# Scores of the cross-attention's heads placed between its query projections

## The chip, the core and the metric

The kernel runs on one core of one Trainium2 chip. The metric is the device time of one execution in microseconds (us). The engines are TensorE (PE; PEld is its weight load, which overlaps), VectorE (DVE), ScalarE (ACT), GpSimd (POOL) and SyncE (SP), which only issues transfers here. Each engine runs its own queue of instructions in order and waits on semaphores that the others raise.

## The reference, cut to what matters

A decoder trunk of two layers over 256 tokens of width 1024. Each layer has a mixer of four head groups, a cross-attention into 256 memory tokens, and a grouped mixture of experts, each followed by a LayerNorm. The change is in the cross-attention:

```python
def memory_cross_attention(x, mem, wq, wk, wv, wo):
    q = (x @ wq).reshape(bsz, s_len, X_HEADS, X_HEAD_DIM)      # 4 heads of 256
    k = (mem @ wk).reshape(bsz, -1, X_HEADS, X_HEAD_DIM)
    v = (mem @ wv).reshape(bsz, -1, X_HEADS, X_HEAD_DIM)
    s = jnp.einsum('bqhd,bkhd->bhqk', q, k).astype(jnp.float32) * (X_HEAD_DIM ** -0.5)
    p = jax.nn.softmax(s, axis=-1).astype(v.dtype)
    o = jnp.einsum('bhqk,bkhd->bqhd', p, v).reshape(bsz, s_len, D_MODEL)
    return o @ wo
```

## The kernel before

**Units.** Every large weight matrix is cut into units of 1 MB. A unit is loaded by SP into one of six `raw` slots, split by ACT into a rounded high half (`hi`, L618: `w_hi`, two instructions) and by DVE into the remainder (`lo`, L903: `w_lo`, two instructions), and used by PE in three products for each pair of operands (L1490 to L1492, `three`). There are two split slots. `ahead(u)` on ACT and on DVE splits unit u+2 as soon as PE has used unit u. The cross-attention of a layer has four value units (`U_V`), four query units (`U_Q`, one for each head: `project("xq0")` to `project("xq3")`) and four output units (`U_O`). SP loads a unit when the unit before it in the same slot has been split; loads of the expert weights follow in the same queue.

**A head of the cross-attention.** `xq{h}`: the query unit, moved out of PSUM by ACT to `qT` (`move`, L641). `cs{h}`: its scores, on PE at L1739, each of four products run as two passes. `x_head_max(h)` on DVE (L1260) gives the row maxima and raises `xmax_ready`. The exponentials on ACT (L782) write `xprobs` and, by a read of the accumulator, the row sums. DVE takes the reciprocal (L1268), multiplies (L1271) and raises `xprobs_ready`. `cpt{h}`: PE transposes the probabilities (L1748, `x_probs_t`), ACT moves them to `xprobsT` (L641). `cpv{h}`: PE multiplies by the values (L1760), ACT moves the result (L641), and DVE splits it (`split_y`, L933 and L935) for the output units, which accumulate in `quad` (L1490 to L1492). In the trace `qT`, `xprobs`, `xprobsT` and the values all show as `arena`, and the keys as `mem_kT`.

**What sets the order.** The order on each engine is written out by hand. PSUM results other than the long accumulations go through four banks (`ring`): `ring_jobs()` lists the jobs of a layer in order with the engine that empties each, job i uses bank i mod 4, and `free` makes PE wait until job i-4 has been emptied. The waits count the jobs that an engine has emptied, so each engine must keep to the order of the list.

**Order before.** PE runs the four query units, then the scores of heads 0 to 3, then `cpt0`, and then for each head `cpt{h+1}` and `cpv{h}`, then the output units. ACT moves `xq0` to `xq3`, with a split (`hi`) after each, and then has the exponentials of heads 0 to 3, `cpt0`, `cpt1`, `cpv0` and so on. DVE splits three units (`lo` of the third and fourth query unit and of the first output unit), then works through maxima and multiplications, and then splits the second output unit.

Of the kernel before, what the change touches and what calls it, by code (L numbers as in the profile page):

```python
# [23 lines left out]
X_HEADS = 4  # L24
# [33 lines left out]
U_Q = U_V + 4  # L58
# [14 lines left out]
def ring_jobs():  # L73

    jobs = [(f"xa{i}", "dve") for i in range(4)]
    jobs += [("cq", "act"), ("ckv", "dve"), ("v", "act"), ("ssq", "dve"), ("ssk", "dve"), ("u", "act"),
             ("rb0", "dve"), ("b", "act")]
    jobs += [(f"q{i}", "act") for i in range(4)]
    jobs += [("kn0", "act"), ("kn1", "act"), ("vv0", "act"), ("vv1", "act"), ("d", "act")]
    jobs += [(f"qt{i}", "act") for i in range(4)]
    jobs += [("wst", "act"), ("c", "act"), ("s0", "act"), ("s1", "act"), ("s2", "act"), ("s3", "act"), ("h", "act")]
    jobs += [(f"mt{i}", "dve") for i in range(4)]
    jobs += [("pt0", "act"), ("pt1", "act"), ("s4", "act"), ("s5", "act"), ("xk0", "act"), ("pv0", "dve"), ("mix", "dve"), ("pt2", "act"), ("pt3", "act"), ("s6", "act"),
             ("s7", "act"), ("xk1", "act"), ("pv1", "dve"), ("pt4", "act"), ("pt5", "act"), ("xk2", "act"),  # L90
             ("yd", "dve"), ("pv2", "dve"), ("pt6", "act"), ("pt7", "act"), ("pv3", "dve"), ("xk3", "act")]
    jobs += [(f"xb{i}", "dve") for i in range(4)]
    jobs += [(f"xq{i}", "act") for i in range(4)]
    jobs += [(f"cs{i}", "act") for i in range(4)]
    jobs += [("cpt0", "act")]
    for i in range(4):
        jobs += ([(f"cpt{i + 1}", "act")] if i < 3 else []) + [(f"cpv{i}", "act")]
    jobs += [("xc0", "act"), ("xc1", "act"), ("rt0", "act"), ("xc2", "act"), ("xc3", "dve"), ("rt1", "act")]
    jobs += [(f"gb{i}", "act") for i in range(8)]
    return jobs  # L100


def hybrid_trunk_kernel(nc, x, mem, positions, w_in, gmlp_v_norm_g, gmlp_w_s, gmlp_b_s, mla_q_norm_g,
# [57 lines left out]
    with ExitStack() as ctx:  # L161
# [114 lines left out]
        xb_hi = rounded("xb_hi", 9216, DC, SEQ)  # L276
        xb_lo = rounded("xb_lo", 0, DC, SEQ)
# [66 lines left out]
        values_moved = sem("values_moved")  # L344
# [259 lines left out]
        def _(act):  # L604
# [85 lines left out]
            for l in range(DEPTH):  # L690
                def ahead(u):

                    hi(u + SPLIT_SLOTS, l, size.get(u + SPLIT_SLOTS, NORMAL))
# [20 lines left out]
                for i in range(4):  # L714
                    t, h = i // 2, 4 * (i % 2)
# [10 lines left out]
                for i in range(4):  # L726
                    t, h = i % 2, 4 * (i // 2)
# [45 lines left out]
                    for a in range(2):  # L773
                        last = nc.scalar.copy(xv[:, t, 512 * a:512 * a + 512], quad[:, 2 * t + a, :])
                last.then_inc(values_moved, 1)
                for i in range(4):
                    move(f"xq{i}", l, qT[:, 2 * i:2 * i + 2, :], bank2(f"xq{i}"), scale=256.0 ** -0.5, unit=U_Q + i)
                    ahead(U_Q + i)
                for h in range(X_HEADS):
                    act.wait_ge(xmax_ready, l * X_HEADS + (h + 1))  # L780
                    for t in range(T):
                        nc.scalar.activation(xprobs[:, h, 256 * t:256 * t + 256],  # L782
                                             bank(f"cs{h}")[:, 256 * t:256 * t + 256], ACT.Exp,
                                             bias=smax[:, h, t:t + 1], accum_out=ssum[:, h, t:t + 1])
                    act.drain().then_inc(act_emptied, 1)
                def x_probs_t(h):
                    if h >= 2:
                        act.wait_ge(misc_ready, misc_done(f"cpv{h - 2}", l))
                    move(f"cpt{h}", l, xprobsT[:, h % 2, :], bank(f"cpt{h}"))

                x_probs_t(0)
                for h in range(X_HEADS):
                    if h + 1 < X_HEADS:
                        x_probs_t(h + 1)

                    move(f"cpv{h}", l, qT[:, 2 * h:2 * h + 2, :], bank2(f"cpv{h}"))
# [101 lines left out]
        def _(dve):  # L898
# [130 lines left out]
            for l in range(DEPTH):  # L1029
# [10 lines left out]
                def ahead(u):  # L1040
                    lo(u + SPLIT_SLOTS, l, size.get(u + SPLIT_SLOTS, NORMAL))
# [211 lines left out]
                x_low("xb", l, 2, None, xb_hi, xb_lo)  # L1253
                for i in range(2, 4):
                    ahead(U_V + i)
                for i in range(3):
                    ahead(U_Q + i)
                def x_head_max(h):
                    dve.wait_ge(misc_ready, misc_done(f"cs{h}", l))
                    nc.vector.tensor_reduce(smax[:, h, :], bank2(f"cs{h}"), AX_X, ALU.max, negate=True)  # L1260
                    dve.drain().then_inc(xmax_ready, 1)

                x_head_max(0)
                for h in range(X_HEADS):
                    if h + 1 < X_HEADS:
                        x_head_max(h + 1)
                    dve.wait_ge(act_emptied, emptied(f"cs{h}", l))
                    nc.vector.reciprocal(srec[:, h, :], ssum[:, h, :])  # L1268
                    dve.drain()
                    for t in range(T):  # L1270
                        nc.vector.tensor_scalar(xprobs[:, h, 256 * t:256 * t + 256], xprobs[:, h, 256 * t:256 * t + 256],  # L1271
                                                srec[:, h, t:t + 1], None, ALU.mult)
                    dve.drain().then_inc(xprobs_ready, 1)
                ahead(U_Q + 3)
                for h in range(X_HEADS):
                    dve.wait_ge(act_emptied, emptied(f"cpv{h}", l))
# [197 lines left out]
        def _(pe):  # L1474
# [106 lines left out]
            for l in range(DEPTH):  # L1581
# [60 lines left out]
                for i in range(2):  # L1642
                    o = free(f"kn{i}", l)
                    for j in range(4):
                        h = 4 * i + j
# [82 lines left out]
                        transpose_x("xb", l, 1)  # L1728
                    into_quad(x_hi, x_lo, 2 * i, 2, U_V + i, l, i == 0, i == 3, values=True)
                pe.wait_ge(dve_emptied, emptied("xb3", l))  # L1730
                for i in range(4):
                    project(f"xq{i}", U_Q + i, l, xb_hi, xb_lo)
                pe.wait_ge(values_moved, l + 1)
                for h in range(X_HEADS):
                    o = free(f"cs{h}", l)
                    pe.wait_ge(act_emptied, emptied(f"xq{h}", l))
                    for t in range(T):
                        for c in range(2):
                            r = mm(o[:, t * 256:(t + 1) * 256], qT[:, 2 * h + c, t * P:(t + 1) * P], kT[:, 2 * h + c, :],  # L1739
                                   start=c == 0, stop=c == 1)  # L1740
                    r.then_inc(misc_ready, 1)
                def x_probs_t(h):
# [6 lines left out]
                                                    ident[:])  # L1749
                    r.then_inc(misc_ready, 1)  # L1750

                x_probs_t(0)
                for h in range(X_HEADS):
                    if h + 1 < X_HEADS:
                        x_probs_t(h + 1)
                    o = free(f"cpv{h}", l)
                    pe.wait_ge(act_emptied, emptied(f"cpt{h}", l))
                    for c in range(2):
                        for m in range(2):
                            r = mm(o[:, c * SEQ:(c + 1) * SEQ], xv[:, m, 256 * h + 128 * c:256 * h + 128 * c + P],  # L1760
                                   xprobsT[:, h % 2, 256 * m:256 * m + 256], start=m == 0, stop=m == 1)
                    r.then_inc(misc_ready, 1)
# [301 lines left out]
```

## Time and profile before

| | |
|---|---|
| median of 3 runs | 774.19 us (770.89 to 776.81) |
| the profiled execution, its own time | 775.23 us |
| span of its core, first to last instruction | 773.4 us |
| mean granted TensorE clock | 0.979 of full speed |
| PE busy | 727.7 us, 94% of the span |
| DVE busy | 400.7 us, 52% |
| ACT busy | 276.4 us, 36% |

The profiled execution takes 1.8 us more than its span; that is what lies before the first and behind the last instruction. Times in the rows are counted from the start of the span. The cross-attention's query units of layer 0 run from 171.7 us, those of layer 1 from 550.2 us.

### The profile page before, as it was taken

To read this page: it belongs to the slowest core of one execution; us is meant where nothing else is said; L and a number is where in the kernel's file an instruction comes from. 1 tells how busy PE (TensorE), PEld (TensorE's weight loads), DVE (VectorE), ACT (ScalarE), POOL (GpSimd) and SP (SyncE) were. 2 spreads that over 40 slices of the span, in tenths; PEclk is the share of its full clock that TensorE was granted. 3 is DMA by queue.
4 is the path that set the end of the run, shared out by engine and by line. 5 is a ranking of instruction groups with operands and counts; after the bars stand their busy time and mean duration, and the time that the engine had idled before them with its cause. 6 is when DMAs were issued, how large, how long until landed. Compare 5 with 4: busy or idle time off the path is not lost.

```text
span 773.4 us, 12363 instructions
## 1 busy us (share of the span) xinstructions
PE 727.7 (94%) x4972; PEld 591.5 (76%) x4972; DVE 400.7 (52%) x701; ACT 276.4 (36%) x473; POOL 46.4 (6%) x88
## 2 busy tenths in 40 slices
PE   3999999999999989999799989999999999899992
PEld 3989897889789965655499789888997898565651
DVE  4685886664537612111558587858444573111115
ACT  4355643444524122111334565335553231211121
POOL 3500000010004200000020000001000010000000
PEclk8999999999999999999999999999999999999996
DMA  8991334573329479999975322456631573899961
GB/s 274 345 316 57 120 124 164 175 244 127 108 91 364 150 278 389 417 415 416 347 262 165 111 96 84 149 184 220 196 109 56 217 328 114 325 412 418 418 271 57
DMA packets 62496, 176.11 MB, mean 228 GB/s; under 512 B 3824, under 2 KB 37024, under 8 KB 53216
## 3 DMA queue, kind: packets, MB, share of 16 engines
q1 hardware_dynamic: 57824, 162.80, 57.0%
q0 software_dynamic: 4032, 12.24, 4.9%
q8 instruction: 43, 0.70, 0.4%
q10 hardware_dynamic: 576, 0.20, 0.1%
q14 instruction: 21, 0.17, 0.1%
HBM read 174.18 MB, written 1.05 MB: 227 GB/s over the span
## 4 chain that ended last, share of the span: by engine, by line
PE 85%; DVE 7%; issue 2%; ACT 2%; DVEq 2%; DMA 1%; ACTq 0%; POOL 0%; POOLq 0%; SPq 0%
PE ring L1882 14%; PE ring L1490 7%; PE ring L1915 7%; PE ring L1491 7%; PE ring L1492 7%; PE quad L1490 6%; PE quad L1491 6%; PE quad L1492 6%; PE quad L1927 4%; PE ring L1760 2%; PE quad L1808 2%; PE quad L1809 1%; PE ring L1532 1%; PE ring L1739 1%; PE ring L1638 1%
## 5 line engine op out<-in xcount | busy, mean ns | idle before, releaser
L903 DVE TENSOR_TENSOR w_lo<-raw,w_hi 128x1024 fp32r<-128x1024 f32 x112 | 132.5, 1222 | 64.6 <-ACT w_hi L618 60.3
L618 ACT CAST w_hi<-raw 128x1024 fp32r<-128x1024 f32 x112 | 111.9, 1049 | 79.5 <-PE quad L1492 70.8
L1490 PE MATMUL ring<-x_hi,w_hi 128*128 128x256 f32 x352 | 103.9, 295 | 6.0 <-issue 4.4
L1491 PE MATMUL ring<-x_lo,w_hi 128*128 128x256 f32 x352 | 101.0, 287 | 0.0
L1492 PE MATMUL ring<-x_hi,w_lo 128*128 128x256 f32 x352 | 100.9, 287 | 0.0
L1490 PEld LDWEIGHTS ring<-x_hi,w_hi 128*128 128x128 f32 x352 | 69.0, 196 | 8.0 <-issue 6.5
L1491 PEld LDWEIGHTS ring<-x_lo,w_hi 128*128 128x128 f32 x352 | 69.1, 196 | 0.7 <-issue 0.5
L1492 PEld LDWEIGHTS ring<-x_hi,w_lo 128*128 128x128 f32 x352 | 68.9, 196 | 0.0
L641 ACT ACTIVATE arena<-ring 128x512 f32<-128x512 f32 (+1 forms) x66 | 35.5, 572 | 86.3 <-PE ring L1492 69.9
L1412 DVE TENSOR_TENSOR y_lo<-ring,y_hi 128x512 fp32r<-128x512 f32 x32 | 22.1, 692 | 72.9 <-ACT y_hi L858 72.9
L1490 PE MATMUL quad<-w_hi,y_hi 128*128 128x512 f32 x144 | 57.1, 397 | 0.0
L1491 PE MATMUL quad<-w_lo,y_hi 128*128 128x512 f32 x144 | 56.2, 390 | 0.0
L1492 PE MATMUL quad<-w_hi,y_lo 128*128 128x512 f32 x144 | 56.1, 389 | 0.0
L1882 PE MATMUL ring<-raw,x_slots 128*64 128x256 f32 x448 | 51.0, 380 | 4.4 <-ACT arena L851 4.4
L1882 PEld LDWEIGHTS ring<-raw,x_slots 128*64 128x64 f32 x448 | 31.7, 137 | 22.2 <-ACT arena L851 4.9
L578 POOL TENSOR_TENSOR lr<-lv,minus_half 128x1 f32<-128x1 f32 x12 | 7.8, 653 | 628.2 <-DVE lv L992 623.1
L1532 PE MATMUL ring<-ident 128*128 128x128 f32 x300 | 37.5, 283 | 4.0 <-issue 4.0
L1532 PEld LDWEIGHTS ring<-ident 128*128 128x128 f32 x300 | 36.1, 198 | 4.6 <-issue 4.5
L1490 PE MATMUL ring<-xb_hi,w_hi 128*128 128x256 f32 x128 | 36.2, 283 | 0.0
L1491 PE MATMUL ring<-xb_lo,w_hi 128*128 128x256 f32 x128 | 36.2, 283 | 0.0
L1492 PE MATMUL ring<-xb_hi,w_lo 128*128 128x256 f32 x128 | 35.9, 281 | 0.0
L858 ACT CAST y_hi<-ring 128x512 fp32r<-128x512 f32 x32 | 18.7, 585 | 41.4 <-PE ring L1915 41.4
(298 smaller groups left out, 1413.7 us busy)
## 6 DMA issues: line engine op xcount, KB each, us to landing
raw<-in_moe_w_gate SPq DMA_DIRECT2D x20, 1024.0 KB, 7.0
raw<-in_moe_w_up SPq DMA_DIRECT2D x16, 1024.0 KB, 8.1
w_raw<-in_moe_w_up SPq DMA_DIRECT2D x16, 1024.0 KB, 10.6
w_raw<-in_moe_w_down SPq DMA_DIRECT2D x16, 1024.0 KB, 11.3
raw<-in_w_in SPq DMA_DIRECT2D x14, 1024.0 KB, 12.2
raw<-in_moe_w_down SPq DMA_DIRECT2D x12, 1024.0 KB, 9.8
raw<-in_w_out SPq DMA_DIRECT2D x10, 1024.0 KB, 5.0
raw<-in_xattn_wk SPq DMA_DIRECT2D x8, 1024.0 KB, 6.5
```

Source lines behind the costliest of these rows:

```text
L618: nc.scalar.copy(unit_slot(u, 0, n)[:, s], raw[:, SLOT[u], s]).then_inc(hi_done, 1)
L641: nc.scalar.activation(dst, src, ACT.Copy, scale=scale).then_inc(act_emptied, 1)
L858: nc.scalar.copy(y_of(y_hi, j, a), out_bank(j, a).rearrange("p (a b) -> p a b", a=2)).then_inc(out_hi, 1)
L903: low = nc.vector.tensor_tensor(unit_slot(u, 1, n)[:, s], raw[:, SLOT[u], s], unit_slot(u, 0, n)[:, s].bitcast(F32), ALU.subtract)
L1412: last = nc.vector.tensor_tensor(y_of(y_lo, j, a), out_bank(j, a).rearrange("p (a b) -> p a b", a=2), y_of(y_hi, j, a).bitcast(F32), ALU.s ...
L1490: mm(out, a_hi, b_hi, start=first, stop=False)
L1491: mm(out, a_hi, b_lo, start=False, stop=False)
L1492: return mm(out, a_lo, b_hi, start=False, stop=last)
L1532: mm(o[:, 0:P], ident[:], ident[:], start=True, stop=True)
L1882: r = mm(ring[of_pair(i), b, 0:FF], slots_of(j // 2)[:, c, at_slot:at_slot + EXPERT_SLOTS], w[i][:, c, :], start=c == 0, stop=c == DC - 1)
L1915: r = mm(out_bank(j, a)[of_pair(i), :], h_t[:, j % 2, c * P:(c + 1) * P][:, of_pair(i)], w[i][:, c, 512 * a:512 * a + 512], start=c == 0, ...
L1927: r = mm(quad[:, 2 * t + a, :], to_token[:, j, t * P:(t + 1) * P], y_of(y, j, a).rearrange("p a b -> p (a b)"), start=j == 0 and i == 0, s ...
```

## The change

Nothing is computed differently and no instruction is added or removed. The order is changed on three engines and in the list of PSUM jobs. PE: `xq0, xq1, cs0, xq2, cs1, xq3, cs2, cpt0, cs3, cpt1, cpv0, cpt2, cpv1, cpt3, cpv2, cpv3`. ACT takes the exponentials of head 0 in front of the move of `xq2`, those of head 1 in front of `xq3`, those of head 2 behind the split that follows `xq3`, and those of head 3 behind the move of `cpt0`. DVE takes the maxima of head 0 in front of the split of the fourth query unit, and the multiplication of head 0 and the maxima of head 1 in front of the split of the first output unit; then come the multiplication of head 1, the maxima of heads 2 and 3, and the multiplications of heads 2 and 3. PE's wait for `values_moved` stands behind `cs3` where it stood in front of `cs0`.

```diff
--- before.py
+++ after.py
@@ -90,11 +90,9 @@
              ("s7", "act"), ("xk1", "act"), ("pv1", "dve"), ("pt4", "act"), ("pt5", "act"), ("xk2", "act"),
              ("yd", "dve"), ("pv2", "dve"), ("pt6", "act"), ("pt7", "act"), ("pv3", "dve"), ("xk3", "act")]
     jobs += [(f"xb{i}", "dve") for i in range(4)]
-    jobs += [(f"xq{i}", "act") for i in range(4)]
-    jobs += [(f"cs{i}", "act") for i in range(4)]
-    jobs += [("cpt0", "act")]
-    for i in range(4):
-        jobs += ([(f"cpt{i + 1}", "act")] if i < 3 else []) + [(f"cpv{i}", "act")]
+    for name in ("xq0", "xq1", "cs0", "xq2", "cs1", "xq3", "cs2", "cpt0", "cs3", "cpt1", "cpv0", "cpt2", "cpv1", "cpt3",
+                 "cpv2", "cpv3"):
+        jobs.append((name, "act"))
     jobs += [("xc0", "act"), ("xc1", "act"), ("rt0", "act"), ("xc2", "act"), ("xc3", "dve"), ("rt1", "act")]
     jobs += [(f"gb{i}", "act") for i in range(8)]
     return jobs
@@ -773,10 +771,10 @@
                     for a in range(2):
                         last = nc.scalar.copy(xv[:, t, 512 * a:512 * a + 512], quad[:, 2 * t + a, :])
                 last.then_inc(values_moved, 1)
-                for i in range(4):
+                def queries(i):
                     move(f"xq{i}", l, qT[:, 2 * i:2 * i + 2, :], bank2(f"xq{i}"), scale=256.0 ** -0.5, unit=U_Q + i)
-                    ahead(U_Q + i)
-                for h in range(X_HEADS):
+
+                def x_exps(h):
                     act.wait_ge(xmax_ready, l * X_HEADS + (h + 1))
                     for t in range(T):
                         nc.scalar.activation(xprobs[:, h, 256 * t:256 * t + 256],
@@ -788,7 +786,19 @@
                         act.wait_ge(misc_ready, misc_done(f"cpv{h - 2}", l))
                     move(f"cpt{h}", l, xprobsT[:, h % 2, :], bank(f"cpt{h}"))
 
+                queries(0)
+                ahead(U_Q)
+                queries(1)
+                ahead(U_Q + 1)
+                x_exps(0)
+                queries(2)
+                ahead(U_Q + 2)
+                x_exps(1)
+                queries(3)
+                ahead(U_Q + 3)
+                x_exps(2)
                 x_probs_t(0)
+                x_exps(3)
                 for h in range(X_HEADS):
                     if h + 1 < X_HEADS:
                         x_probs_t(h + 1)
@@ -1253,17 +1263,12 @@
                 x_low("xb", l, 2, None, xb_hi, xb_lo)
                 for i in range(2, 4):
                     ahead(U_V + i)
-                for i in range(3):
-                    ahead(U_Q + i)
                 def x_head_max(h):
                     dve.wait_ge(misc_ready, misc_done(f"cs{h}", l))
                     nc.vector.tensor_reduce(smax[:, h, :], bank2(f"cs{h}"), AX_X, ALU.max, negate=True)
                     dve.drain().then_inc(xmax_ready, 1)
 
-                x_head_max(0)
-                for h in range(X_HEADS):
-                    if h + 1 < X_HEADS:
-                        x_head_max(h + 1)
+                def x_head_norm(h):
                     dve.wait_ge(act_emptied, emptied(f"cs{h}", l))
                     nc.vector.reciprocal(srec[:, h, :], ssum[:, h, :])
                     dve.drain()
@@ -1271,6 +1276,17 @@
                         nc.vector.tensor_scalar(xprobs[:, h, 256 * t:256 * t + 256], xprobs[:, h, 256 * t:256 * t + 256],
                                                 srec[:, h, t:t + 1], None, ALU.mult)
                     dve.drain().then_inc(xprobs_ready, 1)
+                ahead(U_Q)
+                x_head_max(0)
+                ahead(U_Q + 1)
+                x_head_norm(0)
+                x_head_max(1)
+                ahead(U_Q + 2)
+                x_head_norm(1)
+                x_head_max(2)
+                x_head_max(3)
+                x_head_norm(2)
+                x_head_norm(3)
                 ahead(U_Q + 3)
                 for h in range(X_HEADS):
                     dve.wait_ge(act_emptied, emptied(f"cpv{h}", l))
@@ -1728,10 +1744,7 @@
                         transpose_x("xb", l, 1)
                     into_quad(x_hi, x_lo, 2 * i, 2, U_V + i, l, i == 0, i == 3, values=True)
                 pe.wait_ge(dve_emptied, emptied("xb3", l))
-                for i in range(4):
-                    project(f"xq{i}", U_Q + i, l, xb_hi, xb_lo)
-                pe.wait_ge(values_moved, l + 1)
-                for h in range(X_HEADS):
+                def x_scores(h):
                     o = free(f"cs{h}", l)
                     pe.wait_ge(act_emptied, emptied(f"xq{h}", l))
                     for t in range(T):
@@ -1749,7 +1762,19 @@
                                                     ident[:])
                     r.then_inc(misc_ready, 1)
 
+                def queries(i):
+                    project(f"xq{i}", U_Q + i, l, xb_hi, xb_lo)
+
+                queries(0)
+                queries(1)
+                x_scores(0)
+                queries(2)
+                x_scores(1)
+                queries(3)
+                x_scores(2)
                 x_probs_t(0)
+                x_scores(3)
+                pe.wait_ge(values_moved, l + 1)
                 for h in range(X_HEADS):
                     if h + 1 < X_HEADS:
                         x_probs_t(h + 1)
```

## Rows read from the trace of the kernel before

**Rows 1.** Page of the profile: PE's busy time and the chain that ended last

```profile
PE 727.7 (94%) x4972; PEld 591.5 (76%) x4972; DVE 400.7 (52%) x701; ACT 276.4 (36%) x473; POOL 46.4 (6%) x88
PE 85%; DVE 7%; issue 2%; ACT 2%; DVEq 2%; DMA 1%; ACTq 0%; POOL 0%; POOLq 0%; SPq 0%
```

**Rows 2.** Chain of waits, layer 0: start us, us, what; x is instructions

```profile
194.91 5.19 PE ring L1739 x24
...
201.98 0.69 DVE smax L1260
...
203.86 0.61 ACT arena L641
204.46 0.14 issue
204.60 3.31 PE ring L1760 x8
207.91 0.77 PE ring L1748 x4
208.68 1.73 PE ring L1760 x8
210.41 0.44 PE ring L1748 x4
```

**Rows 3.** Timeline of PE, layers 0 and 1: start, us, what, idle before

```profile
201.65 1.04 PE L1748 MATMUL ring<-ident,arena 128*128 128x128 f32 x8
204.60 3.31 PE L1760 MATMUL ring<-arena 128*128 128x256 f32 x8 [1.91 <-ACT arena L641]
...
583.09 2.93 PE L1760 MATMUL ring<-arena 128*128 128x256 f32 x8 [1.91 <-ACT arena L641]
```

**Rows 4.** Stretches: length, busy of PE, PEld, DVE, ACT, POOL; granted clock; DMA

```profile
188.98:194.74 5.76, 5.76 (x50) 5.76 (x49) 2.36 (x2) 2.48 (x3) 0.00 (x0) 1.00 0.51 181
194.74:201.65 6.91, 6.91 (x34) 6.04 (x33) 3.42 (x9) 5.22 (x14) 0.00 (x0) 1.00 0.33 138
202.70:204.60 1.90, 0.00 (x1) 0.03 (x1) 1.49 (x6) 1.76 (x6) 0.00 (x0) 1.00 0.00 0
204.60:207.70 3.10, 3.10 (x8) 2.38 (x9) 2.44 (x3) 0.34 (x1) 0.00 (x0) 0.57 0.00 0
279.68:281.88 2.20, 0.00 (x1) 0.00 (x1) 0.00 (x0) 2.15 (x5) 0.00 (x0) 1.00 0.99 406
281.88:283.00 1.12, 1.12 (x10) 0.77 (x12) 0.00 (x0) 0.00 (x0) 0.00 (x0) 1.00 1.03 421
```

**Rows 5.** Timeline of ACT, layer 0, around the last two query units

```profile
183.92 1.99 ACT L618 CAST w_hi<-raw 128x1024 fp32r<-128x1024 f32 x2
194.94 0.60 ACT L641 ACTIVATE arena<-ring 128x512 f32<-128x512 f32 x1 [3.28 <-PE ring L1492]
195.44 1.98 ACT L618 CAST w_hi<-raw 128x1024 fp32r<-128x1024 f32 x2
197.42 0.47 ACT L782 ACTIVATE arena<-ring,smax 128x256 f32<-128x256 f32 x1
198.24 0.20 ACT L782 ACTIVATION_READ_ACCUMULATOR arena<-ring,smax 128x1 f32 x1
```

**Rows 6.** Timeline of DVE, layer 0: splits, maxima, reciprocal

```profile
184.99 2.36 DVE L903 TENSOR_TENSOR w_lo<-raw,w_hi 128x1024 fp32r<-128x1024 f32 x2 [3.40 <-ACT w_hi L618]
196.67 0.69 DVE L1260 TENSOR_REDUCE smax<-ring 128x2 f32<-128x512 f32 x1 [3.56 <-PE ring L1739]
199.21 0.17 DVE L1268 RECIPROCAL srec<-ssum 128x2 f32<-128x2 f32 x1
200.19 0.69 DVE L1260 TENSOR_REDUCE smax<-ring 128x2 f32<-128x512 f32 x1
```

**Rows 7.** Stretches of the experts, and SP's issues: start, us, what

```profile
300.00:345.00 45.00, 45.00 (x319) 26.31 (x316) 7.76 (x14) 6.54 (x14) 0.00 (x0) 1.00 1.02 417
...
228.82 0.80 SPq L461 DMA_DIRECT2D raw<-in_moe_w_gate  x2
```

## The prediction, made before the changed kernel was built or run

> **What bounds the kernel now.** I read the page first, for the engine that sets the time. PE is busy in 94% of the span and holds 85% of the chain that ended last [rows 1]: only what shortens PE's queue, or fills a hole in it, can shorten the kernel. So the second view is the chain of waits through the cross-attention of layer 0, for the places where the chain leaves PE. It does so once: behind the scores it goes through DVE's maxima of the last head and ACT's exponentials, to ACT's move of `cpt0`, and returns to PE at 204.60 us [rows 2]. PE's timeline shows the hole: the transposes of heads 0 and 1 are all issued 1.04 us after 201.65 us, and the first `cpv` starts 1.91 us after they end, released by ACT. Layer 1 has the same hole, again 1.91 us [rows 3]. `cpt0` was transposed long before; its move stands behind the exponentials of heads 2 and 3 in ACT's queue, and these wait for scores and maxima. The third view is the table of stretches, for the granted clock. It is 1.00 in the query units, in the scores and in the hole itself, and 0.57 in the 3.1 us behind it [rows 4]: most of that stretch is at 1.2 GHz and the rest at 2.4 GHz.
>
> The chain gives the price of the low clock, since its pieces run from end to end. Eight `cpv` passes take 3.31 us behind the hole and 1.73 us one head later; four transposes take 0.77 and then 0.44 us [rows 2]. That is 1.58 + 0.33 = 1.91 us, with the start of the first product after a wait in it. Hole and clock together hold 1.91 + 1.91 = 3.8 us in a layer. This is the most that the change can take out of one, 7.6 us of 775.2 in two layers, since it neither adds nor removes an instruction.
>
> **The change, part by part.** I follow the three queues of layer 0 in the new order. The prices are: a query unit 5.76 us [rows 4], the scores of a head 6.91/4 = 1.73 us [rows 4], the transposes of a head 0.44 and its `cpv` 1.73 us [rows 2], a move 0.60 us, two `hi` instructions 1.98 us, the exponentials of a head from 197.42 to 198.44 = 1.02 us [rows 5], the maxima 0.69 us, the two `lo` instructions 2.36 us, and reciprocal and multiplication of a head, to the next maxima, 200.19 - 199.21 = 0.98 us [rows 6]. A wait from ACT to PE costs 0.14 us [rows 2]; from PE's last product to ACT's move 0.03 us, as the chain has the fourth query unit end at 194.91 us and the move starts at 194.94 us [rows 2, 5]. The maxima of head 0 start 196.67 - (194.91 + 1.73) = 0.03 us behind its scores [rows 2, 6].
>
> *PE's work.* The same instructions. The scores of heads 0 and 1 move ahead of the third and fourth query unit, which end 3.46 us later, at 194.91 + 3.46 = 198.37 us. No time is added by a change of kind between units: scores began on the beat of the units before (the first stretch ends at 194.74 us and the next has PE busy for all of its 6.91 us [rows 4]). Six more such changes in a layer could cost up to a fill of 0.2 us each, were each to start like the first product after a wait; I take nothing, as the row of that very change shows nothing.
>
> *DVE's queue.* The maxima of head 0 now stand in front of the split of the fourth query unit. This is the one new wait with a projection behind it. The scores of head 0 end at about 183.4 + 1.7 = 185.1 us, the maxima at 185.9 and the split at 188.3 us. It began at 184.99 us before [rows 6], and ACT's half is there at 183.92 + 1.99 = 185.9 us in both orders [rows 5]. PE wants the unit behind `cs1`, at 171.7 + 3 x 5.76 + 2 x 1.73 = 192.4 us: 4.1 us to spare, so it costs nothing; were the maxima later than that, each microsecond would be one of PE's. The maxima of head 1 (about 193.4 us) stand in front of the split of `U_O`, which then ends at 195.8 us; its reader starts at 210 us. Behind it waits SP's load of the second gate unit, 2.7 us later than before; its user comes with the experts, behind all output units, and the next load in SP's queue waits for a later split in both orders, so it costs nothing. The split of `U_O+1` comes behind the multiplication of head 3, at 205.1 us, against a first use at 216 us.
>
> *ACT's queue, head 2.* Behind the fourth query unit ACT moves `xq3` (198.40 to 199.00) and splits `U_O+1` (to 200.88 us). The scores of head 2 end at 198.37 + 1.73 = 200.10, its maxima at 200.82 us, so the exponentials start at 200.9 and end at 201.9 us; the move of `cpt0` follows, to 202.6 us, and `cpv0` may start at 202.74 us. Meanwhile PE has transposed head 0 (normalised since 189 us) to 200.54, run `cs3` to 202.27 and `cpt1` to 202.71 us. ACT and PE arrive together: the hole is gone, to within the 0.2 us of a first product that had to wait.
>
> *The rest.* The maxima of head 3 end at 202.99, its exponentials at 204.07, the move of `cpt1` at 204.77 us, so `cpv1` may start at 204.91 us; PE gets there after `cpv0` (204.6) and `cpt2` (205.1 us; head 2 was multiplied at 204.1 us). From there PE has `cpt3`, `cpv2`, `cpv3`, and each move is ready 0.9 us early or more. The last `cpv` ends at 210.74 us. Before, it ended at 204.60 + 3.31 + 0.77 + 1.73 + 0.44 + 3.46 = 214.31 us; the 3.46 us are two heads at 1.73. The gain is 3.6 us in a layer, if the granted clock stays at 1.00.
>
> *What is late next.* DVE's `split_y` of head 0 is done about 208.9 us, before PE wants it, so the output units start at once, 3.6 us earlier. Their splits follow PE's use of a unit and shift with it. The experts' weights move at 417 GB/s and with PE busy throughout [rows 7]. If that stream were the bound, the gain would be eaten there. But its loads start when the last output units have been split or used (the two issued at 228.82 us [rows 7], and all behind them), so the stream shifts by the same 3.6 us, and PE's stretch of 45.00 us busy in 45.00 us has no wait on it.
>
> *The clock.* The hole had 1.90 us without a product at a granted clock of 1.00, and the low clock came behind it. But a stretch of the experts has PE idle for 2.20 us, and the clock behind that is 1.00 [rows 4]. So a hole of this size can but need not bring the clock down, and a smaller one that remains could do it too; both layers had the drop. The Trainium skill ("TensorE: Matmul & The Clock Gate", section "What's actually happening") says that a monitor sets the clock gate by how busy the engine has recently been. By that rule a queue without the hole keeps the high clock. The trace agrees in that the clock is 1.00 wherever PE was busy without a break before.
>
> **Sum.** 2 x 3.57 = 7.1 us. The profiled execution would come to 775.2 - 7.1 = 768.1 us; from the median of the runs, 774.2 - 7.1 = 767.1 us, 0.92% less. The median lies 1.0 us below the profiled execution, and the three runs spread over 5.9 us, so about 1% (7.7 us) is the least that a measurement of this kernel tells from no change.
>
> **The rivals.**
> *The clock falls all the same, or small waits remain.* For it: ACT and PE meet within 0.1 us at `cpv0` and at 0.2 us at `cpv1`, and the two transposes and `cpv0` are still the place where PE waits if ACT is late. Against it: no hole of over 0.2 us is left by the durations. With only the hole gone the gain is 2 x 1.91 = 3.8 us: 770.4 us.
> *It comes to nothing.* The gain is given back behind the cross-attention, to the stream of weights or to the chains of the LayerNorms. For it: 417 GB/s for 45 us; against it: loads that shift with PE, and no wait of PE on a transfer. 774 us.
> *Slower.* DVE runs its queue in order, and the maxima of head 0 now stand in front of the split that the fourth query unit needs. If they come more than 4.1 us late, PE stalls there, and the time is above that of before from 4.1 + 3.6 = 7.7 us late. A full round of unit, move and scores, 5.76 + 0.60 + 1.73 = 8.1 us, would be such a delay, if the order of bank releases made `cs0` wait for the third unit: 774.2 + 2 x 0.4 = 775 us. Against it: `cs0` takes the bank of `xb2`, emptied before the first query unit can start (PE waits for `xb3` there), and needs only the move of `xq0`, at 171.7 + 5.8 + 0.6 = 178.1 us. The Trainium skill ("TensorE: Matmul & The Clock Gate", section "Architectural detail: the array is 16x 32x32, not 1x 128x128") calls ACT and DVE strictly first in, first out, which is the ground of this rival; DVE's split that waited 3.40 us for ACT with nothing let past it [rows 6] agrees.
> *More than the sum.* The mean granted clock is 0.979, so about 16 us of full clock are missing in the span, and this place holds under 4 of them. An earlier start of the LayerNorms could move another low stretch; one such stretch less is 1.9 us, two are 3.8: 764 us or so.
>
> **How the numbers follow.** The forecast, 767.1 us, has a chance of 0.62; the clock or small waits at 770.4 us 0.19; nothing 0.07; slower 0.04; more than the sum 0.08. The bounds of the forecast itself are 774.2 - 7.6 = 766.6 us and, with a fill of 0.2 us at twelve changes of kind, 767.1 + 2.4 = 769.5 us. The range reaches from 765.5 (half way to the case of more) to 771.5 us, which takes in the first rival with the scatter of a median of such runs. Faster by over 1% means under 766.4 us: the last case and about a third of the forecast, by the scatter, together 0.28. Slower by over 1% would take 7.7 us more; with half the slower case and the scatter, 0.03. Within 1%: 0.69.
>
> **What the new profile would show.** PE's timeline without a wait of over 0.2 us between the first query unit and the output units; the granted clock at 1.00 there; from the first query product to the first output product 38.7 us, where it was 42.25. The maxima of head 0 in front of a split of 2.36 us that ends near 188 us. The first load of experts behind the output units 3.6 us earlier in layer 0, 7.1 us in layer 1. The prediction is wrong if `cpv0` still waits for ACT by over 0.5 us, if the clock there is under 0.9 without such a wait, if the fourth query unit waits for DVE, or if the start of the next layer is not earlier by what the output units are.

## The result, and the profile after

The changed kernel takes 769.23 us (median of 20 runs, 767.78 to 772.09) against 775.14 us (20 runs) for the kernel before on the same chips. The ratio is 0.9932 with a 95% interval of 0.9919 to 0.9945: 5.3 us less, between 4.3 and 6.3. The profiled execution has 769.7 us, a span of 768.0 us and a mean granted clock of 0.984.

The chain that ended last (share of the span by engine) has moved from DVE to PE by two points against [rows 1]:

```profile
PE 87%; DVE 5%; issue 2%; ACT 2%; DVEq 1%; DMA 1%; ACTq 0%; POOLq 0%; SPq 0%; POOL 0%
```

PE's timeline in layer 0 of the changed kernel (start, us, line, what), from the first query product to the first output product. L1752 are the scores, L1761 the transposes, L1785 `cpv`; they answer to L1739, L1748 and L1760 of [rows 2, 3].

```profile
173.19 0.28 PE L1506 MATMUL ring<-xb_hi,w_hi 128*128 128x256 f32 x1
...
203.57 0.60 PE L1761 MATMUL ring<-ident,arena 128*128 128x128 f32 x4
204.22 1.97 PE L1785 MATMUL ring<-arena 128*128 128x256 f32 x8
206.02 0.60 PE L1761 MATMUL ring<-ident,arena 128*128 128x128 f32 x4
206.46 1.89 PE L1785 MATMUL ring<-arena 128*128 128x256 f32 x8
208.19 0.60 PE L1761 MATMUL ring<-ident,arena 128*128 128x128 f32 x4
208.62 3.62 PE L1785 MATMUL ring<-arena 128*128 128x256 f32 x16
211.89 0.58 PE L1506 MATMUL quad<-w_hi,y_hi 128*128 128x512 f32 x1
```

No row shows an idle time in front of it. The first `cpv` starts 0.65 us after the transposes of head 1, where the other two transposes are followed after 0.44 and 0.43 us: ACT came 0.2 us late. From first query product to first output product it is 211.89 - 173.19 = 38.70 us, where it was 42.25; layer 1 has 587.48 - 548.77 = 38.71 us. That is 3.55 us less in each layer (3.54 in the second, where it was 42.25 as well).

The table of stretches (as in [rows 4]) of the changed kernel gives the other half of the story. The second row is the place of the old hole; the 0.87, 1.00 and 0.88 behind the counts in parentheses are the granted clock.

```profile
84.00:97.00 13.00, 11.24 (x82) 10.15 (x82) 9.30 (x22) 6.68 (x16) 0.00 (x0) 0.87 0.45 155
200.00:215.00 15.00, 14.95 (x77) 12.84 (x76) 9.69 (x18) 8.96 (x19) 0.00 (x0) 1.00 0.31 113
460.00:474.00 14.00, 12.51 (x94) 11.39 (x95) 10.19 (x23) 7.66 (x18) 0.00 (x0) 0.88 0.42 150
```

The clock stays at 1.00 in the cross-attention. But 1.76 of the 13.00 us around 90 us are without a product (a hole that both kernels have in the mixer, where PE waits for DVE), and the granted clock is 0.87 there; that execution is 1.5 us behind the one of before when its query units start, in code that the change does not touch. The rest of the way has 0.6 us more between the two cross-attentions (336.88 us from the first output product of layer 0 to the first query product of layer 1, where it was 336.24) and 0.4 less behind the second. So the two spans differ by 5.4 us although the two layers gave 2 x 3.55 = 7.1 us. The question for the runs was whether a single execution misleads here, and in which direction.

ACT and DVE of the changed kernel, layer 0, at the places that the prediction named:

```profile
199.88 0.60 ACT L639 ACTIVATE arena<-ring 128x512 f32<-128x512 f32 x1 [3.98 <-PE ring L1508]
200.37 1.98 ACT L616 CAST w_hi<-raw 128x1024 fp32r<-128x1024 f32 x2
202.36 0.47 ACT L780 ACTIVATE arena<-ring,smax 128x256 f32<-128x256 f32 x1
203.48 0.60 ACT L639 ACTIVATE arena<-ring 128x512 f32<-128x512 f32 x1
```

```profile
186.64 0.69 DVE L1268 TENSOR_REDUCE smax<-ring 128x2 f32<-128x512 f32 x1 [3.56 <-PE ring L1752]
187.45 2.36 DVE L913 TENSOR_TENSOR w_lo<-raw,w_hi 128x1024 fp32r<-128x1024 f32 x2
```

With 1.49 us taken off for the later start, the exponentials of head 2 start at 200.87 us (forecast 200.9), the move of `cpt0` at 201.99 (202.0), the maxima of head 0 at 185.15 (185.1) and the split behind them ends at 188.3 us (188.3).

### The profile page after: what moved, and what is told of

Same layout as the page of the kernel before. It is cut to its first block, busy times and chain, and to the rows that moved or that the text cites. A ratio compares the mean times of both kernels' runs of the same rounds, so it can differ in the third digit from the quotient of the medians.

```text
span 768.0 us, 12363 instructions
## 1 busy us (share of the span) xinstructions
PE 726.6 (95%) x4972; PEld 590.8 (77%) x4972; DVE 400.2 (52%) x701; ACT 276.3 (36%) x473; POOL 46.7 (6%) x88
## 4 chain that ended last, share of the span: by engine, by line
PE 87%; DVE 5%; issue 2%; ACT 2%; DVEq 1%; DMA 1%; ACTq 0%; POOLq 0%; SPq 0%; POOL 0%
PE ring L1907 15%; PE ring L1506 7%; PE ring L1940 7%; PE ring L1507 7%; PE ring L1508 7%; PE quad L1506 6%; PE quad L1507 6%; PE quad L1508 6%; PE quad L1952 4%; PE ring L1548 2%; PE ring L1785 2%; PE ring L1752 2%; PE quad L1833 2%; PE quad L1834 1%; PE ring L1654 1%
## 6 DMA issues: line engine op xcount, KB each, us to landing
w_raw<-in_moe_w_down SPq DMA_DIRECT2D x16, 1024.0 KB, 10.9
```

## The experiments

There are two questions: which part of the edit takes the hole away, and what the low clock behind the hole is worth over many executions. A low stretch is a stretch of time in which the granted clock is at its lower level. Theory 1 says that a low stretch of the clock falls behind a hole of about 2 us only in a part of the executions. Theory 2 says that it always does, and that a part of the gain is given back later. Ratios are to the kernel before, with 95% intervals; microseconds are the ratio's distance from 1 times 775. All diffs are cut to what matters.

**The edit, one half each.** `e2_tail_only` keeps the four query units together and only takes `cpt0` in front of `cs3` (against the changed kernel):

```diff
-    for name in ("xq0", "xq1", "cs0", "xq2", "cs1", "xq3", "cs2", "cpt0", "cs3", "cpt1", ...
+    for name in ("xq0", "xq1", "xq2", "xq3", "cs0", "cs1", "cs2", "cpt0", "cs3", "cpt1", ...
# PE
-                queries(0)
-                queries(1)
+                for i in range(4):
+                    queries(i)
                 x_scores(0)
-                queries(2)
                 x_scores(1)
-                queries(3)
                 x_scores(2)
                 x_probs_t(0)
                 x_scores(3)
# ACT
-                queries(0)
-                ahead(U_Q)
-                queries(1)
-                ahead(U_Q + 1)
+                for i in range(4):
+                    queries(i)
+                    ahead(U_Q + i)
                 x_exps(0)
-                queries(2)
-                ahead(U_Q + 2)
                 x_exps(1)
-                queries(3)
-                ahead(U_Q + 3)
                 x_exps(2)
                 x_probs_t(0)
                 x_exps(3)
# DVE: the order of before
```

> The four query units stay together and the scores behind them, as before; only cpt0 is taken in front of cs3 on PE, and its move in front of the exponentials of head 3 on ACT. By the prediction's own durations cs2 ends at the same time as in the changed kernel, and from there on the queues are the same: the hole is gone and the time is that of the changed kernel, 5 to 7 us less than before. Rival (it is the scores between the units, with the softmax of the first heads beside projections, that takes the hole away): at least half of the gain is missing, 0 to 3 us less than before.

Measured: 770.24 us (6 runs), 0.9945 (0.9928 to 0.9962), 4.3 us less. PE's timeline of `e2_tail_only` (L1746 scores, L1755 transposes, L1777 `cpv`):

```profile
171.73 0.28 PE L1500 MATMUL ring<-xb_hi,w_hi 128*128 128x256 f32 x1
...
202.40 0.60 PE L1755 MATMUL ring<-ident,arena 128*128 128x128 f32 x4
202.84 1.96 PE L1777 MATMUL ring<-arena 128*128 128x256 f32 x8
204.63 0.60 PE L1755 MATMUL ring<-ident,arena 128*128 128x128 f32 x4
205.22 1.97 PE L1777 MATMUL ring<-arena 128*128 128x256 f32 x8
...
210.72 0.58 PE L1500 MATMUL quad<-w_hi,y_hi 128*128 128x512 f32 x1
```

The stage takes 210.72 - 171.73 = 38.99 us, 0.3 more than in the changed kernel and 3.3 less than before. With the scores behind all four units the transposes of head 0 start 0.2 us later (200.18 - 171.73 = 28.45 us behind the first query product, where the changed kernel has 201.41 - 173.19 = 28.22); DVE's multiplication of head 0 ends at 200.09 us there. Its interval, 2.9 to 5.6 us less, reaches the 5 to 7 us that were expected, leaves out nearly all of the rival's 0 to 3, and overlaps that of the changed kernel. So the timing can't tell `e2_tail_only` from the changed kernel; that the hole is gone is shown by the trace.

`e3_units_only` is the other half, again against the changed kernel: the scores stand between the query units, but `cs3` in front of `cpt0` and the exponentials of head 3 in front of its move, as before.

```diff
-    ... "xq3", "cs2", "cpt0", "cs3", "cpt1", ...
+    ... "xq3", "cs2", "cs3", "cpt0", "cpt1", ...
# ACT
                 x_exps(2)
-                x_probs_t(0)
                 x_exps(3)
+                x_probs_t(0)
# PE
                 x_scores(2)
-                x_probs_t(0)
                 x_scores(3)
+                x_probs_t(0)
```

> Scores stand between the query units as in the changed kernel, but cs3 stays in front of cpt0, and ACT has the exponentials of head 3 in front of cpt0's move, as before. By the durations ACT's move of cpt0 then ends 1.7 us behind cpt1 on PE: the hole stays at 1.7 to 1.8 us, and the time is 0 to 1 us less than before. Rival (as above): the hole is mostly gone and the time is within 2 us of the changed kernel.

Measured: 774.99 us (12 runs), 1.0008 (0.9990 to 1.0026). PE's timeline has the hole, now 1.78 us:

```profile
173.30 0.28 PE L1506 MATMUL ring<-xb_hi,w_hi 128*128 128x256 f32 x1
...
203.24 1.04 PE L1761 MATMUL ring<-ident,arena 128*128 128x128 f32 x8
206.05 1.97 PE L1785 MATMUL ring<-arena 128*128 128x256 f32 x8 [1.78 <-ACT arena L639]
...
213.73 0.58 PE L1506 MATMUL quad<-w_hi,y_hi 128*128 128x512 f32 x1
```

So the part that gives the change its name gives nothing that the timing can measure; in the traces it is worth 0.13 us of the hole here and 0.3 us of the stage against `e2_tail_only`. The gain is in two places of the queues, taken together: `cpt0` in front of `cs3` on PE, and its move in front of the last exponentials on ACT. No run changes only one of the two. And this trace has what those of before so far had not: eight passes in 1.97 us right behind the hole. The clock stayed high there, in layer 1 as well. The stage takes 213.73 - 173.30 = 40.43 us in both layers, 1.82 less than before, and yet the span is 773.6 us against 773.4. Outside the stages 3.8 us are lost: 1.6 us ahead of the first query product, 0.7 between the layers and 1.5 behind the second stage, where the row 655 to 670 us now has the low clock:

```profile
460.00:474.00 14.00, 12.23 (x87) 11.12 (x87) 10.41 (x25) 7.68 (x19) 0.00 (x0) 0.88 0.39 133
655.00:670.00 15.00, 12.80 (x100) 9.13 (x99) 1.26 (x4) 3.31 (x7) 0.00 (x0) 0.89 0.67 257
```

That is what theory 2 calls given back, in one execution against one other. It is weak evidence, since three of the six traces of before (below) have the first 1.6 us as well.

**The clock, filled holes.** `e1_fill_hole` keeps the order of before and puts products of the identity, whose result nobody reads, into the hole:

```diff
                     if h + 1 < X_HEADS:
                         x_probs_t(h + 1)
+                    if h == 0:
+                        keep_busy("cpv0", l, 16)
                     o = free(f"cpv{h}", l)
```

> The kernel before, with 16 products of the identity (1.8 us of PE) put into the hole in front of the first cpv; they change no result. PE's order is otherwise that of before, so the hole keeps its length. Theory 1 (the gain is the hole, always there, plus a low stretch of the clock behind it that falls only in part of the executions): the clock stays high behind the filler in every execution, and the time falls by 2 x 1.9 us x the share of executions with the low stretch; with a share near one half, 1.5 to 2.5 us less than before. Theory 2 (the low stretch follows the hole every time, and a part of the changed kernel's gain is given back later): 3.8 us less than before. Rival (the clock has no part in it): no change, or up to 0.5 us more.

Measured: 776.41 us (12 runs), 1.0027 (1.0010 to 1.0044), 2.1 us more. None of the three expectations had this, and the trace shows why: 16 products are 32 passes and take 3.7 us, twice what I had reckoned.

```profile
201.57 1.04 PE L1748 MATMUL ring<-ident,arena 128*128 128x128 f32 x8
202.44 3.74 PE L1532 MATMUL ring<-ident 128*128 128x128 f32 x32
206.01 1.89 PE L1762 MATMUL ring<-arena 128*128 128x256 f32 x8
```

The stage takes 41.99 us in this trace; with the hole open and the clock high behind it, it takes 40.56 us (`l3_before_again` below). So the filler overran by 1.4 us in each layer, 2.9 in all, and 2.1 (0.8 to 3.4) were measured. With the count halved (`e5_fill_fitted`, `keep_busy("cpv0", l, 8)`) it fits:

> The kernel before with 8 products of the identity in the hole in front of the first cpv; one such product is two passes of 0.111 us, so they take 1.8 us and fit the hole of 1.91 us, where the 16 of e1_fill_hole took 3.6 us and lengthened PE's queue by 1.7 us in a layer. That run stood 2.1 us above before where the overrun alone is 3.3 us. Theory 1 (low stretches behind the hole in a part of the executions): 1 to 2 us less than before, no low stretch behind the hole. Theory 2 (the low stretch is there every time): 3.8 us less. Rival (the clock has no part): no change.

Measured: 773.59 us (12 runs), 0.9977 (0.9959 to 0.9994), 1.8 us less (0.5 to 3.2). The filler fits:

```profile
204.02 1.95 PE L1532 MATMUL ring<-ident 128*128 128x128 f32 x16
```

The expectation gave 1.7 and 3.3 us for the overrun of `e1_fill_hole`; by the traces it was 1.4 and 2.9. The clock is at 1.00 behind the fillers of both runs, in both layers. Theory 2's 3.8 us lie outside the interval, and so does no change at all, though only just. The profiled execution is the slowest of the twelve (776.89 us): its two stages are 1.68 us shorter each than before, 40.57 us, but the clock is low behind all four other holes of the two layers. So a low stretch that comes up elsewhere is a second way to get 1.8 us out of 3.4.

`e4_after_filled` puts fillers into two other holes of each layer of the changed kernel, 14 in the mixer and 18 in the experts; `e6_after_fill_fitted` has 7 and 9:

```diff
                 transpose_x("mt", l, None)
+                for _ in range(7):
+                    mm(quad[:, 0, 0:P], ident[:], ident[:], start=True, stop=True)
                 probs_t(0, l)
...
                     turn(0)
+                    for _ in range(9):
+                        mm(ring[:, 2, 0:P], ident[:], ident[:], start=True, stop=True)
                     gate(1)
```

> The changed kernel with products of the identity in two other holes of PE in each layer: 14 of them (1.5 us) in front of the transposes of the first mixer heads, where PE waits 1.7 us for DVE, and 18 (2.0 us) in front of the second gate unit of the experts, where it waits 2.2 us for ACT. They change no result and fit the holes. Theory 1 (low stretches of the clock fall behind any hole of about 2 us in part of the executions): fewer low stretches, a mean granted clock of 0.985 or more, a smaller scatter, and 1 to 3 us less than the changed kernel. Theory 2 (the clock is determined by the kernel alone): the time of the changed kernel to within 0.5 us, or about 1.5 us less in every execution.

> The changed kernel with fitted fillers: 7 products (1.55 us) where PE waits 1.7 us for DVE, 9 (2.0 us) where it waits 2.2 us for ACT, in each layer. e4_after_filled had twice as many and overran by 1.3 and 1.8 us in a layer, 6.2 us in all, yet stood only 2.6 us above the changed kernel. Theory 1: 3 to 4 us less than the changed kernel, about 766 us or a ratio of 0.988 to before, and a mean granted clock near 0.99. Rival (the fillers gave nothing, and the overrun was hidden elsewhere): the time of the changed kernel to within 0.5 us.

Measured: `e4_after_filled` 771.90 us (12 runs), 0.9968 (0.9953 to 0.9982), 2.8 us above the changed kernel, by the same error of count as in `e1_fill_hole`: its fillers overran both holes. `e6_after_fill_fitted` 766.61 us (766.00 to 767.85, 5 runs), 0.9889 (0.9865 to 0.9914): 8.6 us less than before, and 3.3 less than the changed kernel by the two ratios (about 1.2 to 5.4, an estimate from their intervals). It is the fastest version. The mean granted clock was expected at 0.985 or more for `e4_after_filled` and near 0.99 for `e6_after_fill_fitted`; it was 0.988 and 0.986, where the changed kernel has 0.983. Its table of stretches, at the two holes of layer 0 and the two of layer 1:

```profile
84.00:97.00 13.00, 12.80 (x110) 11.81 (x111) 10.78 (x26) 8.24 (x19) 0.00 (x0) 1.00 0.36 105
280.00:294.00 14.00, 14.00 (x112) 9.46 (x114) 2.56 (x5) 2.52 (x5) 0.00 (x0) 1.00 0.87 342
...
460.00:474.00 14.00, 13.79 (x116) 12.53 (x115) 11.15 (x25) 8.15 (x19) 0.00 (x0) 1.00 0.42 148
655.00:670.00 15.00, 15.00 (x120) 9.90 (x118) 3.67 (x6) 3.11 (x6) 0.00 (x0) 1.00 0.81 303
```

**More traces of the kernel before.** If the low stretch is there only sometimes, some executions of one and the same kernel must lack it.

> The kernel before, unchanged, for another trace: theory 1 says that some executions have the low stretch behind one or neither of the two holes, at the same length of hole, 1.91 us; theory 2 says both have it.

> As l1_before_again, a third trace of the kernel before: theory 1, a low stretch behind some of the holes of 1.91 us; theory 2, behind both.

> The kernel before, unchanged, a fourth trace. So far its three traces have the low stretch behind all six holes of 1.91 us, and their spans (773.3 to 775.0 us) belong to the slower two thirds of the executions. Theory 1 needs executions without it: those of 770.4 to 774 us with a mean granted clock of 0.984 or more. A trace of such an execution must show the clock at 1.00 behind one or both holes; if it shows it low behind both, the difference lies elsewhere and theory 1 falls.

> As l3_before_again, a fifth trace, with the same expectations.

> As l3_before_again, a sixth trace, with the same expectations.

Measured: 775.05, 776.76, 775.78, 776.59 and 774.57 us. `l1`, `l2` and `l4` have the low stretch behind both holes. `l3` and `l5` have it in layer 0 only. This refutes "always". None of the last three is one of the faster executions (770.4 to 774 us) in which `l3_before_again` wanted to see the clock stay high, so that test of theory 1 has not been made. PE's timeline of `l3_before_again`, both layers, with the same wait of 1.9 us in front of each:

```profile
206.25 3.52 PE L1760 MATMUL ring<-arena 128*128 128x256 f32 x8 [1.92 <-ACT arena L641]
...
585.86 1.97 PE L1760 MATMUL ring<-arena 128*128 128x256 f32 x8 [1.91 <-ACT arena L641]
```

The same kernel, the same execution, the same hole, and eight passes take 3.52 us once and 1.97 us the other time. Its layer 1 also prices the two terms apart: from the first query product to the first output product it takes 593.53 - 552.97 = 40.56 us. Against 42.25 us a low stretch is worth 1.69 us, and against 38.70 us the hole itself 1.86 us. Layer 1 of `l5_before_again` has 591.84 - 551.26 = 40.58 us. The table of stretches of `l3_before_again`, where the third row is layer 1's cross-attention, shows a low stretch in the experts instead, in layer 0:

```profile
280.00:294.00 14.00, 11.80 (x91) 8.10 (x90) 0.90 (x2) 3.05 (x7) 0.00 (x0) 0.88 0.66 249
460.00:474.00 14.00, 12.22 (x97) 11.50 (x97) 12.30 (x27) 8.79 (x25) 0.00 (x0) 1.00 0.22 76
578.00:594.00 16.00, 14.09 (x74) 12.29 (x73) 11.44 (x24) 8.72 (x25) 0.00 (x0) 1.00 0.25 83
```

I went through all traces by this table of the three holes of each layer. (It leaves out low stretches at other places: all traces have one near 385 us, between the layers, and most have one between 12 and 30 us.) In the six of the kernel before, the clock is low behind the cross-attention's hole 10 times in 12, and behind the other two holes of each layer 6 times in 24. In the five traces where the clock stays high behind `cpt1` in both layers and the other holes are open (the changed kernel, `e1`, `e2`, `e3`, `e5`), the others have it 11 times in 20. The times of the stretches agree: outside the two cross-attention stages the six traces of before take 688.8 to 691.3 us, 690.0 in the mean, and these five take 689.5 to 694.1, 691.6 in the mean. That could be chance, or a low stretch that leaves one hole could come up behind another. `e7_before_others_filled` asks for it: the fillers of `e6_after_fill_fitted` in the kernel before, so that only the cross-attention's hole stays open.

> The kernel before with the fitted fillers of e6_after_fill_fitted (7 and 9 products) in the other two holes of each layer; the hole of the cross-attention stays. Theory 1 (each hole has its own share of executions with a low stretch, whatever the others do): the fillers give here what they gave on the changed kernel, 2.6 us: about 772 us or a ratio of 0.9965. Rival (a low stretch that one hole no longer has comes up behind another, so that with the cross-attention's hole in place the others have fewer): 1.0 stretch in a trace of before outside it, at 1.7 us each, so 1.7 us or less, a ratio of 0.998 or more, and the clock low behind the cross-attention's holes at least as often as before. The two lie 0.9 us apart, so only a clear result at either end tells them apart.

Measured: 771.59 us (6 runs), 0.9954 (0.9938 to 0.9971), 3.6 us less (2.2 to 4.8); in its trace the clock is low behind the cross-attention's hole in layer 0 and not in layer 1. This fits theory 1: its 2.6 us lie in the interval, and the fillers give about as much with the cross-attention's hole open (3.6 us) as without it (3.3 us), as far as intervals of over 2 us can tell. The rival's 1.7 us or less lie outside. What the run does not test is the other direction: whether closing the cross-attention's hole brings low stretches up elsewhere.

## Why the prediction was right, and where its size was off

The direction, the mechanism and the range held; the size was 7.1 us where 5.3 (4.3 to 6.3) were measured. Of the 2.1 us between the forecast time of 767.1 us and the measured 769.23, about 0.9 come from its base: the median of three runs, 774.19 us, was 775.14 over twenty. The range was wide enough to take in the first rival (770.4 us) too, so the time alone does not confirm the mechanism; the traces and the two halves of the edit do. By its steps:

- *Where the chain leaves PE.* Right: the hole is at `cpt0`'s move, and `e3_units_only` and `e2_tail_only` show that the order of `cpt0` against `cs3` and of its move against the exponentials of head 3 decides it.
- *The queues of the new order.* Right to 0.1 us at every place read above; 38.70 us against a forecast of 38.7, and the wait at `cpv0` of 0.2 us as allowed for. DVE's maxima in front of the fourth query unit's split cost nothing, so the slower rival had no ground: PE has no wait in the stage.
- *What I did not see.* My own walk had the exponentials of head 2 start behind maxima that follow `cs2`, which ends at the same time whether the scores stand between the units or behind them. It follows that the scores' new places gain next to nothing, which `e3_units_only` showed (0.3 us in a layer by the traces, nothing in the timing). The prediction never set its order against the smaller swap, and so did not say which part of the edit earns the gain.
- *What is late next.* Right: the first expert load behind the output units is issued at 226.78 us in the trace, 2.04 us earlier than in [rows 7], which is 3.53 us with the later start of 1.49 taken off. Nothing is given back in the stream of weights there. The sign named last, the start of the next layer, came short of it: the first query product of layer 1 is 550.19 - 548.77 = 1.42 us earlier, 2.9 with the later start taken off, not 3.55, and the first output product of layer 1 is 592.44 - 587.48 + 1.49 = 6.5 us earlier by the same count, not 7.1. The way between the two stages took 336.88 us; the six traces of before have 336.24 to 337.37, so the 0.6 us are within what one and the same kernel shows.
- *The clock.* This is the mis-sized term. The step "hole and clock together hold 1.91 + 1.91 = 3.8 us in a layer" took a low stretch from one trace and counted it for every execution. A low stretch is worth 1.69 us, not 1.91; this alone is small, since the prediction's 1.91 us held the start of a first product after a wait, as it said. But it is not there every time. The holes are sure: 2 x 1.86 = 3.7 us. That leaves 5.3 - 3.7 = 1.6 us (0.6 to 2.6) for two low stretches that would give 3.4. Two accounts fit. By the first, a low stretch stands behind the hole in about half of the timed executions. By the second, it stands there as often as in the traces, 10 times in 12, which gives 2.8 us, and about 1 us of that is lost to low stretches elsewhere; the 1.6 us more outside the stages speak for it (691.6 against 690.0 us), with a scatter as large as themselves. The fillers do not choose: `e5_fill_fitted`, which takes only the clock's part, gives 1.8 us (0.5 to 3.2), which holds both 1.7 and 2.8, and `e1_fill_hole` gives 2.9 - 2.1 = 0.8 us (nothing to 2.1), nearer to the first account or to a larger loss elsewhere.
- *The mean granted clock does not choose either.* It is 0.9812 over 46 timed executions of before and 0.9829 over 20 of the changed kernel. But it counts all of the span. Behind the last product PE has nothing to do, and the six traces of before have 8.9 to 10.9 us of low clock there, the changed kernel 13.3 (estimates from stretches of 4 us). The 16 us of full clock that the prediction found missing hold 5 of this kind, which no change of PE's work can win back. Executions of the changed kernel with 0.981 took 767.8 to 768.6 us, one with 0.984 took 770.2.
- *The hint was there.* The prediction held the hole of 2.20 us in the experts with a clock of 1.00 behind it against its own price, and wrote that a hole "can but need not" bring the clock down. It then took the drop as certain in both layers, because both showed it. A weight of one half for that term would have given 2 x (1.86 + 0.85) = 5.4 us, but nothing on record then gave the weight.

What stays open is which of the two accounts holds. Six profiled executions of before are few, and their times (774.6 to 776.8 us) lie in the slower part of 770.4 to 777.4; whether that is chance, or profiled executions differ, no run tells. Why the clock falls behind a hole in one layer and not in the other is open too.

## What to carry to other kernels

When a chain leaves the bounding engine, look for the instruction that comes back to it and for what stands ahead of that one in its own queue; the cheapest cure can be to swap these two; here the larger reordering around it added at most 0.3 us in a layer. Run each half of an edit alone. Do not count a low stretch of TensorE's clock from a single trace as a term of every execution: price the hole, and the low stretch with a share, and take several traces of the same kernel. Count the low stretches stage by stage, in the stages that the change does not touch too: the mean granted clock also counts time in which the engine has nothing to do. A short hole that can't be closed can be filled with products nobody reads, as long as their passes are counted from the trace: the fitted fillers gained, and those of twice the length cost more than they gave.

## What the runs showed that I had not expected

Behind the same wait of 1.9 us, with the same kind of work before it, the granted clock fell to the lower level in layer 0 and stayed at the upper in layer 1 of one execution (3.52 against 1.97 us for eight passes). Fitted fillers were worth 1.8 us (0.5 to 3.2) in the cross-attention's hole alone and 3.3 and 3.6 us in the other two kinds, although they add work to an engine that is busy for 94% of the span. And `e3_units_only` has stages 1.82 us shorter than before without a shorter span, since in that trace its low stretches stand elsewhere. Last, a product of two 128x128 matrices in f32 is two passes of 0.11 us, so `keep_busy` with 16 products is 3.6 us of PE (206.01 - 202.44 in `e1_fill_hole`), not 1.8.
